# Sending the expert weights of a mixture layer as 1 MB instead of 2 MB transfers

## The reference, cut to what matters

```python
def hier_moe(h, w_group, b_group, w_router, b_router, w_gate, w_up, w_down):
    ...
    for gi in range(N_EXPERT_GROUPS):
        hid = (jax.nn.silu(jnp.einsum('td,edf->tef', ht, w_gate[gi]))
               * jnp.einsum('td,edf->tef', ht, w_up[gi]))
        y = y + jnp.einsum('tef,efd->td', hid * cw[:, gi, :, None], w_down[gi])
```

## Time and profile before

| | |
|---|---|
| median of the three executions | 1615.34 us (1610.56 to 1615.7) |
| the profiled execution, its own time | 1613.04 us |
| span of the profiled execution, from the first to the last instruction | 1610.9 us |
| granted TensorE clock, mean over the span | 0.975 |
| TensorE matmul busy | 1520.2 us (94%) |
| weight load 860.1 us, VectorE 673.8 us, ScalarE 231.4 us, GpSimd 34.8 us | |
| moved by transfers | 589.91 MB, 366 GB/s over the span |

### The profile page before, as it was taken

One profiled execution on the slowest core, in us unless ns is written; L12 is line 12 of the kernel. 1 busy time (PEld: TensorE's weight loads), 2 busy tenths in 40 slices (PEclk: granted clock), 3 DMA queues, 4 the chain that ended last, 5 costly groups with the idle time before them and its releaser, 6 DMA issues.

```text
span 1610.9 us, 19379 instructions
## 1 busy us (share of the span) xinstructions
PE 1520.2 (94%) x7856; PEld 860.1 (53%) x7856; DVE 673.8 (42%) x1201; ACT 231.4 (14%) x441; POOL 34.8 (2%) x55
## 2 busy tenths in 40 slices
PE   4899999999999998899999999999999999999996
PEld 2778888855555445554455455455455445444442
DVE  1674667675777643322423223232232232332323
ACT  2000312111223303010110110111011011010012
POOL 2000000000001200000000000000000000000001
PEclk8899999999999999799999999999999999999998
DMA  9999477699767995589999999999999999999993
GB/s 360 383 359 369 149 297 269 257 361 355 274 261 280 345 408 211 242 336 417 428 429 429 428 429 428 428 430 429 427 429 427 429 430 429 427 430 427 429 429 146
DMA packets 97790, 589.91 MB, mean 366 GB/s; under 512 B 5440, under 2 KB 7968, under 8 KB 72400
## 3 DMA queue, kind: packets, MB, share of 16 engines
q1 hardware_dynamic: 95376, 580.93, 88.7%
q0 software_dynamic: 1696, 5.66, 1.0%
q10 hardware_dynamic: 672, 2.66, 0.4%
HBM read 587.07 MB, written 2.16 MB: 366 GB/s over the span
## 4 chain that ended last, share of the span: by engine, by line
PE 84%; DMA 8%; DVE 3%; SPq 2%; issue 1%; ACT 1%; ACTq 0%; DVEq 0%
PE bank L1015 26%; PE bank L1042 13%; PE bank L961 7%; PE bank L865 7%; PE bank L985 6%; PE bank L619 5%; DMA ring<-in_w_up 4%; PE bank L653 4%; PE bank L582 3%; PE bank L823 3%; DMA ring<-in_w_ada 3%; SPq L361 2%; PE bank L632 1%; PE bank L635 1%; DMA RX<-in_x 1%
## 5 line engine op out<-in xcount | busy, mean ns | idle before, releaser
L1015 PE MATMUL bank<-ring,RN 128*64 128x512 f32 x2000 | 440.3, 592 | 1.0 <-DMA ring<-in_w_up 1.0
L1015 PEld LDWEIGHTS bank<-ring,RN 128*64 128x64 f32 x2000 | 169.8, 137 | 258.3 <-issue 252.9
L1042 PE MATMUL bank<-ring,RN 128*64 128x512 f32 x1024 | 228.5, 598 | 16.6 <-issue 16.6
L1974 DVE TENSOR_TENSOR RN<-bank,RN 64x512 f32<-64x512 f32 x32 | 22.2, 693 | 372.9 <-ACT RN L1351 372.9
L1042 PEld LDWEIGHTS bank<-ring,RN 128*64 128x64 f32 x1024 | 85.1, 137 | 137.9 <-issue 137.9
L1981 DVE COPY RG<-bank 64x512 f32<-64x512 f32 x64 | 44.1, 689 | 234.0 <-PE bank L1042 233.5
L961 PEld LDWEIGHTS bank<-RN,RX 128*128 128x128 f32 x1024 | 118.5, 196 | 14.5 <-issue 13.0
L961 PE MATMUL bank<-RN,RX 128*128 128x128 f32 x1024 | 121.7, 281 | 1.4 <-DVE RN L1915 1.4
L985 PE MATMUL bank<-RG,RN 128*128 128x512 f32 x256 | 114.1, 599 | 1.6 <-DVE RG L1981 1.6
L865 PE MATMUL bank<-ring,RT 128*128 128x512 f32 x256 | 113.0, 601 | 0.8 <-DVE RT L1805 0.8
L582 PE MATMUL bank<-RH,ring 128*128 128x256 f32 x448 | 105.3, 400 | 7.4 <-ACT RH L1134 7.4
(11 more groups left out here) (351 smaller groups left out, 1142.3 us busy)
## 6 DMA issues: line engine op xcount, KB each, us to landing
ring<-in_w_down SPq DMA_DIRECT2D x64, 2048.0 KB, 13.7
ring<-in_w_up SPq DMA_DIRECT2D x63, 2048.0 KB, 17.9
ring<-in_w_gate SPq DMA_DIRECT2D x62, 2048.0 KB, 13.6
ring<-in_w_ada SPq DMA_DIRECT2D x32, 2048.0 KB, 10.3
ring<-in_w_in SPq DMA_DIRECT2D x19, 2048.0 KB, 9.2
ring<-in_w_ada SPq DMA_DIRECT2D x32, 1024.0 KB, 14.5
ring<-in_w_out SPq DMA_DIRECT2D x8, 2048.0 KB, 13.7
ring<-in_w_in SPq DMA_DIRECT2D x8, 1792.0 KB, 13.0
```

The source lines that it names most:

```text
L1015: last = mm(bank[0][64 * s:64 * s + 64, :], tokT[:, k, q * CAP:(q + 1) * CAP], w[:, k % 8, :], start=k == 0, stop=k == KT - 1, skip_group_ ...
L1042: last = mm(bank[2 + n % 2][64 * (n // 2):64 * (n // 2) + 64, :], hidT[:, k * CAP:(k + 1) * CAP], wdn[:, n * BLK:(n + 1) * BLK], start=k = ...
```

## The change

Each 2 MB piece is sent as two transfers of 1 MB: the first 8 KB and the last 8 KB of each partition's 16 KB. The places in memory stay as they were, and so do the matmuls and their order. Each half has a landing semaphore of its own (`expert_landed0a`, `expert_landed0b`, ...). TensorE waits for the halves at `k` = 0, 4, 8, 12 of gate and up and before each of the four steps of down, and raises `expert_used` after each half, so that it counts 12 for each expert (`PIECES`). SyncE sends in the order in which TensorE uses: gate a, up a, gate b, up b of slots 0 and 1, the same of slots 2 and 3, then 4a, 4b, 5a, 5b, each behind its own wait. All other users of `expert_used` wait for the count that stands for the same point as before.

```diff
+PIECES = 2 * HB
...
+            def send_halves(dst, src, names):
+
+                for h in range(2):
+                    c = slice(2048 * h, 2048 * h + 2048)
+                    sp.dma_start(dst[:, c], src[:, c]).then_inc(sig(names[h]).sem, 16)
+
             for s in (1, 0, 2, 4, 3, 5):
-                wait(sp, f"freed{s}", len(SLOT_LOADS[s]))
-                sp.dma_start(dst_of(s), expert_halves(0)[s]).then_inc(sig(f"expert_landed{s}").sem, 16)
+                sp.wait_ge(sig(f"freed{s}").sem, len(SLOT_LOADS[s]))
+                send_halves(dst_of(s), expert_halves(0)[s], [f"expert_landed{s}a", f"expert_landed{s}b"])
...
-            def next_piece(e, s, used_of):
-
-                wait(sp, "expert_used", used_of * HB + (s + 1))
-                sp.dma_start(dst_of(s), expert_halves(e)[s]).then_inc(sig(f"expert_landed{s}").sem, 16)
-
-            for s in range(HB):
-                next_piece(2 if s < 3 else 1, s, 0)
-            for s in range(3, HB):
-                next_piece(2, s, 1)
+            def used_pieces(s, h):
+
+                return 4 * (s // 2) + 2 * h + s % 2 + 1 if s < 4 else 8 + 2 * (s - 4) + h + 1
+
+            def next_pieces(e, ss, used_of):
+
+                for s0 in ss:
+                    for h in range(2):
+                        for s in ((s0, s0 + 1) if s0 < 4 else (s0,)):
+                            sp.wait_ge(sig("expert_used").sem, used_of * PIECES + used_pieces(s, h))
+                            c = slice(2048 * h, 2048 * h + 2048)
+                            sp.dma_start(dst_of(s)[:, c], expert_halves(e)[s][:, c])\
+                                .then_inc(sig(f"expert_landed{s}{'ab'[h]}").sem, 16)
...
             with sp.Fori(3, NE) as e:
-                for s in range(HB):
-                    next_piece(e, s, e - 1)
+                next_pieces(e, (0, 2, 4, 5), e - 1)
...
-                        if k % 8 == 0:
+                        if k % 4 == 0:
                             for s in range(2):
-                                n = 2 * (k // 8) + s
+                                n, h = 2 * (k // 8) + s, "ab"[k // 4 % 2]
                                 if ahead and n < 3:
-                                    wait(pe, f"ahead_landed{n}", 16)
+                                    wait(pe, f"ahead_landed{n}{h}", 16)
                                 elif n < 3 and not first:
-                                    pe.wait_ge(sig(f"expert_landed{n}").sem, e * 16)
+                                    pe.wait_ge(sig(f"expert_landed{n}{h}").sem, e * 16)
                                 else:
-                                    pe.wait_ge(sig(f"expert_landed{n}").sem, e * 16 + 16)
+                                    pe.wait_ge(sig(f"expert_landed{n}{h}").sem, e * 16 + 16)
...
-                            if k % 8 == 7:
+                            if k % 4 == 3:
                                 last.then_inc(sig("expert_used").sem, 1)
...
                     for k in range(4):
-                        if k % 2 == 0:
-                            pe.wait_ge(sig(f"expert_landed{4 + k // 2}").sem, e * 16 + 16)
+                        pe.wait_ge(sig(f"expert_landed{4 + k // 2}{'ab'[k % 2]}").sem, e * 16 + 16)
...
-                        if k % 2 == 1:
-                            last.then_inc(sig("expert_used").sem, 1)
+                        last.then_inc(sig("expert_used").sem, 1)
```

More of the change, by code:

```diff
@@ L470, in _ @@
             ahead = [w.rearrange("p k c -> p (k c)") for w in AHEAD]
-            sp.dma_start(ahead[0], expert_halves(1)[0]).then_inc(sig("ahead_landed0").sem, 16)
-            wait(sp, "x2_ready", 8)
-            sp.dma_start(ahead[1], expert_halves(1)[1]).then_inc(sig("ahead_landed1").sem, 16)
+            send_halves(ahead[0], expert_halves(1)[0], ["ahead_landed0a", "ahead_landed0b"])
+            sp.wait_ge(sig("x2_ready").sem, 8)
+            send_halves(ahead[1], expert_halves(1)[1], ["ahead_landed1a", "ahead_landed1b"])
@@ L474, in _ @@
             wait(sp, "logits1")
-            sp.dma_start(ahead[2], expert_halves(1)[2]).then_inc(sig("ahead_landed2").sem, 16)
-            def next_piece(e, s, used_of):
-                wait(sp, "expert_used", used_of * HB + (s + 1))
-                sp.dma_start(dst_of(s), expert_halves(e)[s]).then_inc(sig(f"expert_landed{s}").sem, 16)
-            for s in range(HB):
-                next_piece(2 if s < 3 else 1, s, 0)
-            for s in range(3, HB):
-                next_piece(2, s, 1)
+            send_halves(ahead[2], expert_halves(1)[2], ["ahead_landed2a", "ahead_landed2b"])
@@ new lines, in next_piece @@
+            def next_piece(e, s, h, used_of):
+                sp.wait_ge(sig("expert_used").sem, used_of * PIECES + used_pieces(s, h))
+                c = slice(2048 * h, 2048 * h + 2048)
+                sp.dma_start(dst_of(s)[:, c], expert_halves(e)[s][:, c]).then_inc(sig(f"expert_landed{s}{'ab'[h]}").sem, 16)
+            for h in range(2):
+                next_piece(2, 0, h, 0)
+                next_piece(2, 1, h, 0)
+            for h in range(2):
+                next_piece(2, 2, h, 0)
+                next_piece(1, 3, h, 0)
@@ L486, in _ @@
+            for s in (4, 5):
+                for h in range(2):
+                    next_piece(1, s, h, 0)
+            for h in range(2):
+                next_piece(2, 3, h, 1)
+            for s in (4, 5):
+                for h in range(2):
+                    next_piece(2, s, h, 1)
             with sp.Fori(3, NE) as e:
-                for s in range(HB):
-                    next_piece(e, s, e - 1)
+                next_pieces(e, (0, 2, 4, 5), e - 1)
             wait(sp, "flag_ready")
@@ L492, in _ @@
             over = nc.sync.value_load(flag[0:1, 0:1], min_val=0, max_val=2 * S)
-            wait(sp, "expert_used", NE * HB)
+            wait(sp, "expert_used", NE * PIECES)
             with sp.If(over > 0):
@@ L1349, in _ @@
                     e = p * 2 + q
-                    act.wait_ge(sig("expert_used").sem, e * HB + 4)
+                    act.wait_ge(sig("expert_used").sem, e * PIECES + 8)
                     fn(sil[64:128, :], bank[0][0:64, :], ACT.Silu).then_inc(sig("silu").sem, 1)
@@ L1357, in _ @@
                        ACT.Copy).then_inc(sig("hiddenT_copied").sem, 1)
-                    act.wait_ge(sig("expert_used").sem, e * HB + 6)
+                    act.wait_ge(sig("expert_used").sem, e * PIECES + PIECES)
                     for n in range(2):
@@ L1978, in pair @@
                         tokens(p + 2)
-                    dve.wait_ge(sig("expert_used").sem, e * HB + 6)
+                    dve.wait_ge(sig("expert_used").sem, e * PIECES + PIECES)
                     for n in range(2):
@@ L1991, in _ @@
             pair(1, True, first=True)
-            wait(dve, "expert_used", 2 * HB)
+            dve.wait_ge(sig("expert_used").sem, 2 * PIECES)
             for tt in range(TT):
```

## The result

The changed kernel takes 1619.8 us (median of ten executions, 1617.86 to 1623.87), the kernel before 1611.97 us over ten (1609.69 to 1615.7). The ratio is 1.0044, with a 95% interval of 1.0033 to 1.0055: **0.44% slower**. Forecast were 6.6 us more on a base of 1615.34 us, a ratio of 1.0041. The medians alone differ by 7.8 us, 0.49%, which is inside that interval. The profiled execution took 1618.32 us with a span of 1616.3 us.

The account below looks back on a forecast made before the run. The prediction took weight transfers as the bound, narrowly slower than TensorE. A 12.1 us packet loss less gains of 1.8 and 3.5, with 0.2 of rounding, gave +6.6 us: 1622 us, forecast 1616 to 1627, range with rivals 1612 to 1632.

Parts of the forecast that it names:

- The bound: Expert loop: transfers slower than TensorE by 0.27 us an expert; a 6.0 us lead hides it; all waiting costs 1.9 us.
- The size of packets: Expert weight stream: 8 KB packets instead of 16 KB lower the rate from 428 to 422 GB/s, a loss of 12.1 us.
- The gains: 3.5 us from halves of expert 31's last gate and up pieces; 1.8 us from an earlier first full-stream issue.
- The sum: End of expert 31's gate and up: loss 12.1, gains 1.8 and 3.5, 0.2 of rounding, giving +6.6 us.
- the point at which the lead ends: Expert loop: rounds of 58.26 us until about expert 19, near 1210 us, and of 59.6 us from there on.
- The absolute time: Whole kernel: 1619.6 us for the profiled execution, 1622 us with the 2.3 us between it and the median.
- The waits: TensorE's gate and up waits for transfers grow from 1.9 to about 8 us, all at step 12, none in down.
- The extra waits on TensorE: More waits and releases in TensorE's gate and up and down steps: cost zero.
- A: Rival: transfer rate stays, 8 KB packets lose nothing measurable; 1613.4 us, not slower; chance 0.17.
- B: Rival: transfer rate falls as in the 4 or 7 KB rows, 416 or 412 GB/s; 1634 or 1643 us; chance 0.09.
- C: Rival: each transfer has a cost; 0.1 us uncovered for each of 348 adds 35 us, 1657 us; chance 0.02.
- D: Rival: something else helps, such as less memory contention or longer full clock; below 1610 us; chance 0.04.

Follow-up runs that it names:

- e8: Kernel before with gate and up rows of four steps side by side in main memory, waited for and released every four steps, packets still 16 KB: ratio 0.9981.
- e5: Kernel before with 256 unread bytes after every 8 KB of expert weights in main memory, so packets are 8 KB and transfers stay 2 MB: ratio 1.0084.
- e6: Kernel before with 256 unread bytes after every 16 KB of expert weights in main memory, so packets stay at 16 KB: ratio 0.9999.
- e9: Kernel before with each 2 MB piece sent as two 1 MB transfers, even and odd partitions, packets still 16 KB: ratio 1.0006.
- e3: Changed kernel with TensorE waiting for both halves of its pieces at once, releases still fine: ratio 1.0071 of the kernel before.
- e10: Changed kernel with fine waits, but used places reported only as often as in the kernel before: ratio 1.0053 of the kernel before.
- e2: Kernel before with each 2 MB piece sent as two 1 MB transfers, lower and upper 64 partitions, packets still 16 KB: 1995 to 2444 us.
- e1: Kernel before with each partition's 16 KB named as two adjoining 8 KB runs inside one 2 MB transfer: ratio 1.0003.

## Why the prediction was right

*The bound.* Right: the transfers were the slower of two nearly equal resources, by 0.27 us an expert, and TensorE lived on a lead. e8 confirms from the other side that all waiting before the change was 1.9 us, because it removes just that.

*The size of packets.* Right, and the term that decides the sign. 422 GB/s was taken from lines through the rows of other sizes, and 422 was measured; 12.1 us were forecast for the stream and e5 has 12.8 (11.8 if e6 is taken for its base). That this belongs to packets and not to transfers was the weaker part of the argument (equal rates of 1 MB and 2 MB transfers at 2 KB packets). e9 and e5 show it directly, by doubling one and keeping the other. That 8 KB runs at steps of 32 KB suit the memory less isn't the cause either: in e5 the runs lie 8.25 KB apart, and the rate is the same.

*The gains.* 3.5 and 1.8 us were forecast, 3.8 and 1.4 measured (e3, e10). Their sum of 5.2 us is right to 0.1, in part by luck: one came out 0.3 too large and the other 0.4 too small.

*The sum.* +6.6 us forecast, +7.8 measured in the stretch and between the medians. The missing 1.2 us, from the profile after: the stream from the first issue (712.80 us) to expert 31's last up half (1582.11 us) took 869.3 us, 0.9 more than the 864.7 + 3.7 of the forecast; the last four steps take 3.67 us and not 3.5; and the issue comes 1.97 us after the start of down where I had about 1.9. The 0.9 come from the rounded rates. 325.65 and 320.61 MB in 760 us are 428.5 and 421.9 GB/s; at these the movement is 851.6 us before and 865.0 us after, a loss of 13.4 us where the forecast has 12.1, and what remains beside the movement did not grow (4.7 us before, 4.3 us after). The same shortfall moved the point at which the lead ends: expert 17 at 1155 us instead of about expert 19 at 1210.

*The absolute time.* 1622 us were forecast and 1619.8 measured, because 1615.34 us, the median of three executions of the kernel before, lay 3.4 us above the median of ten. The base was 3.4 us too high and the change 1.2 us too small, so that the time looks nearer than its base was. In the profiled executions most of the spread arises ahead of the experts: they reach expert 3 at 745.5 to 751 us. For the three executions no profile shows where it arose.

*The waits.* Their place is right: from expert 18 on at step 12 (the x16 rows of the chain) and none in down. Their sum is 839.13 - 829.37 = 9.8 us, against 8.3 forecast. The list of waits shows less, 6.5 us on TensorE, because it has only the idle time: after a wait the last four steps take 3.67 us, and without one they take 13.73 / 4 = 3.43, so that 14 experts lose about 3.4 us more. *The extra waits on TensorE* cost nothing: 13.73 us for the 64 records, as before.

*The rivals.* A fell with the rate; B too, 8 KB is on the line. C, a cost for each transfer, is refuted by e9. D didn't show: TensorE's rounds are 58.26 us as before (746.79 to 805.05 us in the chain after). The rule of the Trainium skill, page "DMA: Bandwidth & Descriptors", section "Rules for kernel authors", asks for 128 partitions and at least 1 MiB per transfer for the highest bandwidth. The changed kernel's transfers fulfil it and reach 422 GB/s, where those of 2 MB reach 428, so that here it isn't enough. Its size limit by itself agrees with the trace (e9: 429 GB/s at 1 MB, though with 64 partitions in a transfer); what it leaves out is the size of packets. The fixed 2.0 us of one transfer (same page, "Anatomy of one DMA"), which the prediction used, is stated there for transfers that GpSimd issues, and SyncE issues these; it can't be seen in a full queue.

## What to carry to other kernels

When a transfer is cut so that TensorE can start earlier, look at what the cut does to the contiguous run of each partition: here a fixed part of about 9 ns a packet took 1.5% of the bandwidth at 8 KB for 16, and 4% at 4 KB, while twice the number of transfers was free. Where the transfers are already the slower resource, that is paid over the whole stream and the finer wait is earned only once, at its end; put what is needed together side by side in main memory instead, so that pieces get finer in use and not in packets. And count first what all the waiting costs (rounds without waits against the stretch): here it was 1.9 us, and no finer cut could have won more.

## What the runs showed of the hardware that was not expected

Two things. A transfer to 64 neighbouring partitions ran at 244 GB/s, one to 64 even or odd partitions at 429 GB/s, with packets of 16 KB in both (e2, e9). What in the chip the neighbours share was not tried further. And two runs that adjoin in both memories became one packet, although the transfer named them apart: e1's two runs of 8 KB left 22,368 packets for 325.70 MB, while 256 unused bytes between the runs on one side (e5) kept them apart. Whether the chip or the building of the program joins them isn't shown.
